# Second attention: in the third and seventh step the query piece leaves its bank ahead of the transposed block and the maximum

## The reference

```python
q = (c_q @ w_uq).reshape(B, S, MLA_HEADS, MLA_NOPE + MLA_ROPE)      # 16 heads, 64 + 32
q_nope, q_rope = q[..., :MLA_NOPE], _rope(q[..., MLA_NOPE:], pos)
kv = (c_kv @ w_ukv).reshape(B, S, MLA_HEADS, MLA_NOPE + MLA_V)       # 64 + 64
k_nope, v = kv[..., :MLA_NOPE], kv[..., MLA_NOPE:]
for qb in range(S // 128):                                           # 8 query blocks
    q0, n_keys = qb * 128, qb * 128 + 128
    s = (q_nope[q0:n_keys] . k_nope[:n_keys] + q_rope[q0:n_keys] . k_rope[:n_keys]) * scale
    p = _masked_softmax(s, _chunk_mask(q0, n_keys))
    outs.append(p @ v[:n_keys])
```

## Time and profile before

| | |
|---|---|
| median of three runs | 2898.34 us |
| profiled execution | 2890.08 us, span of its instructions 2888.4 us |
| TensorE matmul busy | 2649.1 us (92%) |
| VectorE busy | 1557.7 us (54%) |
| ScalarE busy | 1168.0 us (40%) |
| GpSimd busy | 436.6 us (15%) |
| mean granted TensorE clock | 0.974 of full speed |
| the 16 heads of the second attention | about 1552 to 2052 us of the span |

### The profile page before, as it was taken

One profiled execution on the slowest core, in us unless ns is written; L12 is line 12 of the kernel. 1 busy time (PEld: TensorE's weight loads), 2 busy tenths in 40 slices (PEclk: granted clock), 3 DMA queues, 4 the chain that ended last, 5 costly groups with the idle time before them and its releaser, 6 DMA issues. The chain is left out here.

```text
span 2888.4 us, 36971 instructions
## 1 busy us (share of the span) xinstructions
PE 2649.1 (92%) x12454; PEld 2173.6 (75%) x12454; DVE 1557.7 (54%) x2537; ACT 1168.0 (40%) x2071; POOL 436.6 (15%) x440
## 2 busy tenths in 40 slices
PE   3899989879999999999997888888799999999997
PEld 2677777757788888887766777777577888888886
DVE  4577777747754443443765566566376323232346
ACT  2366656534512213123454666666246122131224
POOL 0000000001110010051143544444110000000000
PEclk8999999989999999999999999999899999999999
DMA  8233333263342241321341111111633111111123
GB/s 319 77 98 101 109 91 109 78 234 93 102 138 88 80 131 51 117 80 57 89 132 23 36 30 25 35 29 35 226 95 88 59 50 51 44 51 51 44 88 102
DMA packets 325470, 255.20 MB, mean 88 GB/s; under 512 B 40647, under 2 KB 290806, under 8 KB 324350
## 3 DMA queue, kind: packets, MB, share of 16 engines
q1 hardware_dynamic: 309550, 195.26, 23.2%
q0 software_dynamic: 14736, 50.34, 5.6%
q10 hardware_dynamic: 1088, 8.39, 0.7%
HBM read 216.17 MB, written 33.59 MB: 86 GB/s over the span
## 5 line engine op out<-in xcount | busy, mean ns | idle before, releaser
L1832 PE MATMUL PA<-U,W 128*128 128x512 f32 x3840 | 950.2, 402 | 68.4 <-DVE H L1723 51.0
L1832 PEld LDWEIGHTS PA<-U,W 128*128 128x128 f32 x3840 | 725.9, 191 | 239.2 <-DVE H L1723 37.3
L782 ACT ACTIVATE W<-raw 128x1024 fp32r<-128x1024 f32 (+2 forms) x262 | 260.0, 994 | 817.5 <-PE PA L1832 389.8
L1832 PE MATMUL SC<-U,W 128*128 128x512 f32 x2064 | 482.3, 392 | 10.3 <-DMA U<-attention_out 6.5
L1832 PEld LDWEIGHTS SC<-U,W 128*128 128x128 f32 x2064 | 387.8, 188 | 96.9 <-DMA U<-attention_out 7.1
L1832 PE MATMUL PA<-H,W 128*128 128x512 f32 x1536 | 359.1, 392 | 3.2 <-DVE W L1244 3.2
L1832 PE MATMUL SC<-H,W 128*128 128x512 f32 x1536 | 355.3, 390 | 0.0
L1244 DVE TENSOR_TENSOR W<-raw,W 128x1024 fp32r<-128x1024 f32 x232 | 286.9, 1237 | 103.5 <-ACT W L782 102.3
L1832 PEld LDWEIGHTS PA<-H,W 128*128 128x128 f32 x1536 | 288.3, 188 | 64.3 <-DVE W L1244 3.6
L1832 PEld LDWEIGHTS SC<-H,W 128*128 128x128 f32 x1536 | 288.1, 188 | 60.7 <-issue 1.0
L580 POOL DMA_DIRECT2D ada<-in_ada_w x80 | 57.9, 724 | 873.3 <-DVE acc L1258 869.8
(11 more groups left out here) (245 smaller groups left out, 3097.8 us busy)
## 6 DMA issues: line engine op xcount, KB each, us to landing
raw<-in_ffn_w SPq DMA_DIRECT2D x160, 512.0 KB, 4.0
ada<-in_ada_w POOLq DMA_DIRECT2D x80, 512.0 KB, 4.5
U<-attention_out SPq DMA_DIRECT2D x4, 3584.0 KB, 17.5
raw<-in_da_w_qkv SPq DMA_DIRECT2D x24, 512.0 KB, 5.1
ada_first<-in_ada_w ACTq DMA_DIRECT2D x4, 2048.0 KB, 18.1
H<-H SPq DMA_DIRECT2D x32, 256.0 KB, 5.1
attention_out<-ostage SPq DMA_DIRECT2D x32, 256.0 KB, 2.9
raw<-in_da_w_o SPq DMA_DIRECT2D x16, 512.0 KB, 3.9
```

The lines of the kernel that those rows point to most:

```text
L782: nc.scalar.activation(W[:, slot, 0, 0:kt * P], raw[:, slot, 0:kt * P], ACT.Copy).then_inc(w_hi, 1)
L1832: ins = mm(bank, W[:, slot, a, kt * P:(kt + 1) * P], moving(b, kt)[:, cols], start=kt == first and (a, b) == SPLIT[0], stop=kt == last and ...
```

## The change

In ScalarE's and VectorE's `heads1` of the second attention, in step 2 and step 6, the query piece is taken ahead of the transposed groups: on ScalarE the copy stands behind the exponential and ahead of the high parts, on VectorE the three instructions stand ahead of the first low part and of the maximum. Step 4, whose piece is keys and values, is as before. TensorE, GpSimd and SP are untouched, and no wait, buffer or instruction is added or removed.

```diff
@@ ScalarE, heads1 @@
                     if s == 1:
                         v_hi(h, p)
+                    if s in (2, 6) and proj:
+                        copy_piece(1 - p, h + 1, s // 2 - 1, PA[0])
                     p_hi(h, p, s, 0)
                     if s >= 4:
                         p_hi(h, p, s, 1)
                     if s == 0 and not is_first(h):
                         copy_piece(p, h, 3, PA[0])
-                    if s in (2, 4, 6) and proj:
-                        copy_piece(1 - p, h + 1, s // 2 - 1, PA[0])
+                    if s == 4 and proj:
+                        copy_piece(1 - p, h + 1, 1, PA[0])
@@ VectorE, heads1 @@
                     if s == 1:
                         v_lo(h, p)
+                    if s in (2, 6) and proj:
+                        lo_piece(1 - p, h + 1, s // 2 - 1, PA[0])
                     p_lo(h, p, s, 0)
                     if s + 2 < NQ:
                         max1(h, s + 2)
@@
                         p_lo(h, p, s, 1)
                     if s == 0 and not is_first(h):
                         lo_piece(p, h, 3, PA[0])
-                    if s in (2, 4, 6) and proj:
-                        lo_piece(1 - p, h + 1, s // 2 - 1, PA[0])
+                    if s == 4 and proj:
+                        lo_piece(1 - p, h + 1, 1, PA[0])
```

## The result

| | before | after |
|---|---|---|
| median | 2898.32 us (4 runs, 2893.29 to 2898.93) | 2916.25 us (4 runs, 2912.44 to 2917.15) |
| ratio | | 1.0061, 95% interval 1.0049 to 1.0074 |
| profiled execution | 2890.08 us, clock 0.974 | 2917.15 us, clock 0.973 |

The change makes the kernel 17.9 us slower, and the interval of the ratio lies clear of 1. 2920.8 us was forecast, with 2903 to 2942 as the range. In the changed kernel the lines behind the edits are 2 to 4 higher: L1725 frees the bank, L1720's and L1721's multiplications are L1722 and L1723, low parts L1337, the maximum L1732, transposes L1843, inverses L2226, projections L1836.

What follows compares the result with a forecast made beforehand. TensorE was taken as busiest, but held in each head by the chain maximum, exponential, high part, low part. (1.17 + 0.33) x 15 heads = +22.5 us on 2898.34 gave 2920.8 us, range 2903 to 2942.

Steps and rivals of the forecast that it cites:

- The mechanism, third step: At s = 2, projection 1.57 us earlier, but maximum 1.80 us late and inverse transposes 1.17 us late: +1.17 us per head.
- The mechanism, seventh step: At s = 6, low part 1.59 us late, first transposes wait about 2.4 us, projection wait gone: +0.33 us per head.
- ScalarE's 0.15 us: In the third step, ScalarE's high part starts 0.15 us later because the query piece's copy goes first.
- the moves costed at nothing: GpSimd's rotation 1.6 to 1.8 us earlier, ScalarE's step 6 parts moved at most 0.2 us, SP unaffected: no cost.
- The sum: Both step balances over heads 0 to 14: (1.17 + 0.33) x 15 = +22.5 us.
- The episodes: Half-clock stretches (1.2 instead of 2.4 GHz) in the heads, 1.5 us each: about eight, 12 us in all, kept unchanged.
- The rival that had more of them: Longer TensorE idle in step 7 and at the inverses brings 7 to 22 more half-clock episodes: 2932 to 2955 us, chance 0.22.
- The 8.26 us between profile and median: Timed median lies 8.26 us above the profiled execution of 2890.08 us; carried over as a constant to the changed kernel.
- The rivals of gain and no change: Gain: projection waits go, delays stay hidden, 2857.8 us, chance 0.07. No change: only +0.33 us per head, 2903.3 us, chance 0.07.
- The page that spoke for a gain: Trainium skill's rule to start the blocking dependency sooner, applied to the 40.8 us projection wait; it pointed to a gain.

Runs made afterwards that it cites:

- the second pair: The kernel before and the changed kernel, each run once more unaltered for its profile: 2897.03 us and 2915.06 us.

## Why the prediction was right

- **The mechanism, third step.** Right. The projection wait is gone, the maximum is late, three waits stand where the last head has them. Forecast were waits of 0.4, 0.7 and 1.6 us, and 0.53, 0.48 and 1.54 us came. The term was +1.17, and it is +1.27 us in the kernel with this step alone. The maximum was to come 1.80 us late, and it came 1.89. VectorE started the piece 0.13 us behind the end of ScalarE's copy (1736.03 + 0.59 to 1736.75), where I had taken 0.03 us from a low part behind a high part; that is the missing 0.1. In the seventh step the same pair takes 0.03 us (1720.77 + 0.59 to 1721.39), so what takes 0.13 in the third is open.
- **The mechanism, seventh step.** Right, with the size off: +0.33 forecast, +0.19 measured. The wait of 2.4 us is there (2.38). The step left out that a projection that doesn't wait lets its successor start some 0.1 us sooner.
- **ScalarE's 0.15 us and the moves costed at nothing.** The kernel with ScalarE's part alone has +0.16 us per head, so this holds. TensorE waits for GpSimd once in the stage, 0.4 us, as before.
- **The sum.** 15 x (1.17 + 0.33) = 22.5 against 15 x 1.47 = 22.1 us, both errors nearly cancelling.
- **The episodes.** This is the term that made 2920.8 instead of 2916.3. I kept their cost. It went from 429.56 - 14 x 29.85 = 11.7 us to 446.19 - 14 x 31.32 = 7.7 us, 4.0 us less, and 22.1 - 4.0 = 18.1 us is the measured 17.9. So close a fit is partly luck, since one pair of profiles does not fix the number of episodes. From the stage's entry to the last head's inverses the changed kernel takes 500.21 us (1560.26 to 2060.47) and the kernel before 482.18 (1552.77 to 2034.95), which is 18.0 us apart. In the second pair it is 500.23 (1560.63 to 2060.86) against 486.06 us (1559.62 to 2045.68), 14.2 us apart, since the kernel before had its 3.4 us more of half clock in the first head there. So the episodes' part of the total is known to a few microseconds only. The rival that had more of them, because TensorE idles longer, took the sign wrong here. It would have been right for the kernel with the piece behind the low part and ahead of the maximum, which has one in every head. (Of that rival's 0.22 the range left out its upper half, which is 0.11 and not the 0.07 that was written.)
- **The 8.26 us between profile and median.** I carried it over as a constant, and the sum against the median stands. As a constant of profiling it was wrong: the second profiled execution of before takes 2900.61 us, 3.6 above its median, about as much as its first head was longer, and the changed kernel's is 0.9 us above. Had I read the sum against the first profiled execution alone, 6.9 us of its luck ahead of the stage would have been in it.
- **The rivals of gain and no change.** Both fall. The 0.28 and 0.80 us waits had said that a late low part would be felt, and it was: TensorE waits 1.54 us for the one where it had waited 0.28, and 2.38 us for the other where it had waited 0.80.
- **The page that spoke for a gain.** The change took the largest gap away entirely, 40.8 us, and the kernel lost 17.9 us. With the same aim, but part of the work put into VectorE's own idle time, it gained 39 us. The Trainium skill, page Perfetto Trace Analysis, section Optimization Strategy, says to make the blocking dependency start sooner or finish faster: by that rule alone both would be gains, and only the second is.

## What to carry to other kernels

The largest wait in a list is not what its removal is worth: before moving the work that ends it, look at what that work overtakes, and who waits for the overtaken ones. An instruction that stands behind a maximum or another handover may be free there because a second engine's turn covers it; moved ahead of the handover it delays all that follows by nearly its full length (here the maximum by 1.89 us for a piece of 2.04), and all that is won back is the part that had stuck out before (0.63 us). Split such a block by what each instruction really needs, and put the ones that need least into the idle time of their own engine.

## What the runs showed of the hardware

- The half-clock episodes don't grow with TensorE's idle time in a simple way. Per head TensorE waited about 2.4 us with the cosine rows first, 3.8 in the kernel before, 4.9 in the changed one and 6.0 with the piece behind the low part and ahead of the maximum; over the 14 intervals the episodes cost 0, 12 and 8 us, and in the last case some 1.5 us in every head. In two executions of the changed kernel they come in every third head at the same places. What decides where they fall stays open.
- Their cost in the kernel before is nearly the same in two executions over the 14 intervals (11.7 and 12.1 us), though they fall on other heads. Ahead of the intervals the two differ by 3.4 us.
- VectorE reads the cosine rows from the same bank of which ScalarE has yet to copy other rows, and TensorE works on the next banks meanwhile; it takes 0.69 us as it did behind the maximum.
